# First mixer rebuilt: modulation as feature columns on turned tokens, full-row weight loads, linear attention's projections first

## What is computed

```python
mod = jax.nn.silu(c) @ w_ada[l] + b_ada[l]
sh1, sc1, gt1, sh2, sc2, gt2 = [m[:, None, :] for m in jnp.split(mod, 6, axis=-1)]
h = rms_norm(x, g_pre_mix[l]) * (1 + sc1) + sh1
y = hybrid_mixer(h, w_in[l], w_gla_gate_up[l], b_gla_gate[l], g_gla_norm[l], sinks[l], w_out[l])
x = x + gt1 * rms_norm(y, g_post_mix[l])
...
def hybrid_mixer(h, w_in, w_gla_gate_up, b_gla_gate, g_gla_norm, sinks, w_out):
    proj = h @ w_in
    aq, ak, av, gq, gk, gv, gg, ga = split_cols(proj, IN_SPLITS)
    att = sliding_window_sink_attention(...)
    glog = jax.nn.log_sigmoid((ga @ w_gla_gate_up + b_gla_gate).astype(jnp.float32)) / GLA_GATE_NORMALIZER
    o = gla_chunked(...)
    o = rms_norm(o, g_gla_norm).reshape(B, S, GLA_V_WIDTH).astype(h.dtype) * jax.nn.silu(gg)
    return jnp.concatenate([att.astype(h.dtype), o], axis=-1) @ w_out
```

## Time and profile before

| | before |
|---|---|
| median of three runs | 1823.8 us (1819.25 to 1826.76) |
| the profiled execution's own time | 1822.55 us |
| its span, first to last instruction | 1820.8 us |
| TensorE busy | 1702.5 us (94%) |
| VectorE, ScalarE busy | 670.8 us (37%), 494.4 us (27%) |
| moved from HBM | 575.06 MB, 316 GB/s over the span |
| end of the first mixer's last product | 210.7 us into the span |
| first expert pass | 259.2 us into the span |
| last expert pass ends | about 1246 us into the span |

### The profile page before, as it was taken

How to read it: one execution, slowest core, us unless ns; L and a number is a source line. 1 busy time by engine, 2 the same in 40 slices (tenths; PEclk the granted TensorE clock), 3 DMA queues, 4 the chain that set the end, 5 groups by cost and what they waited for, 6 DMA issues and landing times.

```text
span 1820.8 us, 22575 instructions
## 1 busy us (share of the span) xinstructions
PE 1702.5 (94%) x9016; PEld 960.6 (53%) x9016; DVE 670.8 (37%) x975; ACT 494.4 (27%) x696; POOL 23.1 (1%) x55
## 2 busy tenths in 40 slices
PE   4987679999999999999999999997999999999998
PEld 0873533333333333333333333335999887789997
DVE  2544532222121221212222121216555556765554
ACT  2333302121111211112121111114333444453333
POOL 2000100000000000000000000000000000000000
PEclk8898769999999999999999999998999999999999
DMA  9665739999999999999999999996655563446551
GB/s 358 210 221 208 284 149 429 428 429 428 429 429 428 429 428 429 429 428 430 427 429 429 428 430 428 428 428 216 201 186 183 178 212 117 162 148 202 185 184 68
DMA packets 117739, 576.74 MB, mean 317 GB/s; under 512 B 8016, under 2 KB 66416, under 8 KB 91328
## 3 DMA queue, kind: packets, MB, share of 16 engines
q1 hardware_dynamic: 113440, 564.22, 77.4%
q0 software_dynamic: 2512, 9.28, 1.5%
q10 hardware_dynamic: 1744, 2.63, 0.4%
HBM read 575.06 MB, written 1.05 MB: 316 GB/s over the span
## 4 chain that ended last, share of the span: by engine, by line
PE 65%; DMA 24%; DVE 7%; ACT 2%; issue 2%; DVEq 0%; SPq 0%; ACTq 0%
DMA ring<-in_w_mlp 22%; PE PS L627 22%; PE PS L912 18%; PE PS L899 7%; PE PS L969 6%; PE PS L669 3%; PE PS L892 1%; PE PS L860 1%; DMA ring<-in_w_ada 1%; PE PS L564 1%; PE PS L877 1%; DVE scr L1848 1%; DVE scr L1854 1%; DVE scr L1851 1%; PE PS L906 1%
## 5 line engine op out<-in xcount | busy, mean ns | idle before, releaser
L912 PE MATMUL PS<-ring,scr 128*64 128x512 f32 x2176 | 501.8, 615 | 9.1 <-DMA ring<-in_w_mlp 9.1
L912 PEld LDWEIGHTS PS<-ring,scr 128*64 128x64 f32 x2176 | 149.3, 135 | 342.9 <-issue 313.4
L1878 DVE TENSOR_TENSOR w_lo<-ring,w_hi 128x2048 fp32r<-128x2048 f32 x90 | 206.2, 2291 | 140.3 <-ACT w_hi L1370 140.0
L899 PE MATMUL PS<-ring,scr 128*64 128x512 f32 x1088 | 248.5, 598 | 0.0
L627 PE MATMUL PS<-HT_hi,w_hi 128*128 128x256 f32 (+1 forms) x784 | 223.4, 285 | 2.6 <-DVE HT_lo L1563 2.6
L627 PE MATMUL PS<-HT_hi,w_lo 128*128 128x256 f32 (+1 forms) x784 | 222.8, 284 | 0.0
L627 PE MATMUL PS<-HT_lo,w_hi 128*128 128x256 f32 (+1 forms) x784 | 222.7, 284 | 0.0
L1370 ACT ACTIVATE w_hi<-ring 128x2048 fp32r<-128x2048 f32 x90 | 172.2, 1913 | 169.8 <-PE PS L627 101.0
L1319 ACT ACTIVATE scr<-scr 64x512 f32<-64x512 f32 x68 | 42.3, 623 | 494.8 <-DVE scr L1847 494.8
L1836 DVE TENSOR_SCALAR scr<-iota,scr 128x128 f32<-128x128 f32 (+1 forms) x68 | 20.5, 343 | 416.1 <-PE PS L912 416.1
L1847 DVE TENSOR_SCALAR scr<-PS 64x512 f32<-64x512 f32 x68 | 46.4, 683 | 336.8 <-PE PS L912 335.6
(11 more groups left out here) (313 smaller groups left out, 1673.9 us busy)
## 6 DMA issues: line engine op xcount, KB each, us to landing
ring<-in_w_mlp SPq DMA_DIRECT2D x204, 2048.0 KB, 21.5
ring<-in_w_ada SPq DMA_DIRECT2D x24, 1024.0 KB, 11.2
ring<-in_ffn_w_gate SPq DMA_DIRECT2D x22, 1024.0 KB, 5.3
ring<-in_ffn_w_up SPq DMA_DIRECT2D x22, 1024.0 KB, 5.3
ring<-in_ffn_w_down SPq DMA_DIRECT2D x22, 1024.0 KB, 4.8
ring<-in_w_in SPq DMA_DIRECT2D x19, 1024.0 KB, 5.1
ring<-in_w_out SPq DMA_DIRECT2D x8, 1024.0 KB, 5.3
ring<-in_w_gate SPq DMA_DIRECT2D x8, 1024.0 KB, 5.1
```

The source lines that it names most:

```text
L899: mm = pe.matmul(PS[c * CAP:(c + 1) * CAP, 6, :], aT[:, h, k, :], w[:, k, c * HALF:(c + 1) * HALF], start=(h == 0 and k == 0), stop=(h == ...
L912: mm = pe.matmul(PS[c * CAP:(c + 1) * CAP, 4 + h, :], xsT[:, 2 * (j % 2) + k, j // 2, :], w[:, k, h, c, :], start=False, stop=(j == 3 and ...
L1878: dve.tensor_tensor(w_lo[:, at % PAIRS, :], raw(n), w_hi[:, at % PAIRS, :].bitcast(F32), ALU.subtract).then_inc(lo_ready, 1)
```

## The change

1. Modulation parts are taken in pairs: a chunk of `w_ada` is now one row block of 2048 columns (128 x 2048, 8 KB in one piece per partition, where it was two pieces of 4 KB), and one pair of parts is eight chunks. There are 24 chunks as before. `ada_part` does four products per chunk as before.
2. Parts 0 and 1 no longer become rows on all partitions. `c`, the gain and the two bias rows are loaded as 32 short rows and turned once by TensorE; the sums are turned by four products (L747), so that shift and scale are columns over the features. The tokens are turned first, after the bare `rsqrt` scale, and the scale and shift are then one VectorE instruction for each block of 128 features (L1703), followed by the two halves of the split. The first projection takes the feature blocks one by one as they come.
3. Parts 2 to 5: the spreading product uses a row of ones and one partition of `apart` instead of `pick`. `apart` exists three times. The products of parts 2 to 5 (16 chunks) stand in the gaps of attention's units 2 to 5, and their sums between the chunks of `w_out`.
4. The projections' order: linear attention's queries, gate, keys and values first, with its steps between the further projections; then attention, with the two chunks of the output gate in units 0 and 1. Values and output gate are taken as half-row chunks with 512 columns per product (24 products a chunk) instead of 48 with 256.
5. `w_out` is taken in the order 2, 3, 0, 1, with waits for the two kinds of head apart.
6. The raw ring has five slots instead of seven, and there are three `w_hi`/`w_lo` pairs instead of two; the memory is the same. The experts' first loads wait for the slots that lie below them, so four of the first six now wait for the end of `w_out`, where it was three.
7. Pool makes `ident` before its small loads, and loads the experts' biases only after the last modulation sum.

```diff
-RAW1, PAIRS1 = 7, 2
+RAW1, PAIRS1 = 5, 3
...
-        def chunks_mix1():
-            ada = lambda m: [two_rows(w_ada, j, m * D) for j in range(4)]
-            win = [columns(w_in, 256 * c) for c in range(5)] + [columns(w_in, 2304, RANK)] + \
-                [columns(w_in, 256 * c) for c in range(5, 9)]
-            return ada(0) + ada(1) + win[:3] + ada(2) + win[3:] + ada(3) + ada(4) + ada(5) + \
-                [two_rows(w_out, j) for j in range(4)]
+        ADA = lambda i, ks=range(KC): [("ada", i, k) for k in ks]
+        PROJ = [("gq",), ("ga",), ("gk",), ("gv", 0), ("gv", 1), ("akv",), ("aq", 0), ("aq", 1), ("gg", 0), ("gg", 1)]
+        OUT = [("out", 2), ("out", 3), ("out", 0), ("out", 1)]
+
+        LOAD1 = ADA(0, range(5)) + PROJ[:2] + ADA(0, range(5, KC)) + PROJ[2:] + ADA(1) + ADA(2, range(4)) + \
+            OUT[:2] + ADA(2, range(4, KC)) + OUT[2:]
+        USE1 = ADA(0) + PROJ + ADA(1) + ADA(2) + OUT
...
+            def ada_part(i, ks, bank):
+                for k in ks:
+                    n = in1("ada", i, k)
                     arrived(n)
+                    for g in range(4):
+                        mm = pe.matmul(PS[32 * g:32 * g + 32, bank, :], cb[:, k, :], raw(n)[:, g * HALF:(g + 1) * HALF],
+                                       start=(k == 0), stop=(k == KC - 1))
                     mm.then_inc(weights_used, 1)
...
+            ada_part(0, range(5, KC), 0)
+            pe.wait_ge(ada_sb, 1)
+            for s in range(4):
+                mm = pe.transpose(PS[:, 1, s * P:(s + 1) * P], apart[0][:, s * P:(s + 1) * P], ident[:])
+            mm.then_inc(ada_ps, 1)
+            hi, lo = split(in1("gq"), 8)
+            for k in range(KC):
+                pe.wait_ge(ht_lo, k + 1)
+                for b, bank in enumerate((0, 3)):
+                    cols = slice(b * P, (b + 1) * P)
+                    for x, w in ((HT1_hi, hi), (HT1_hi, lo), (HT1_lo, hi)):
+                        mm = pe.matmul(PS[:, bank, 0:S], w[:, k, cols], x[:, k, :], ...)
...
+            def beside(u):
+                if u < 2:
+                    two_tiles("gg", u, 0)
+                    if u == 0:
+                        pe.wait_ge(gla_dve, G_OG)
+                else:
+                    i, part = u // 2, u % 2
+                    pe.wait_ge(ev1_act, 2 + i)
+                    ada_part(i, range(4 * part, 4 * part + 4), i - 1)
+            attention(0, beside)
...
+            out_rows(2)
+            ada_sum(3)
+            out_rows(3)
+            ada_sum(4)
+            pe.wait_ge(s_olo, 2)
+            out_rows(0)
+            ada_sum(5)
+            out_rows(1)
...
+            for k in range(KC):
+                dve.tensor_scalar(vb[:, k, :], PS[:, 4 + k // 2, (k % 2) * S:(k % 2 + 1) * S], gsT[:, k:k + 1],
+                                  mod0[:, k:k + 1], ALU.mult, ALU.add).then_inc(v_ready, 1)
+                if k:
+                    low_token(k - 1)
```

More of the change, by code:

```diff
@@ L1249, in _ @@
-            attention(0, HT1_hi, project)
             act.wait_ge(gla_pe, 1)
@@ L1617, in probs @@
                     dve.tensor_tensor(s3, s3, inv.unsqueeze(2).to_broadcast([P, nh, W]), ALU.mult).then_inc(s_p[z], 1)
-                masked(0)
-                masked(1)
+                for u in range(2):
+                    masked(u)
+                    first(u)
                 for u in range(NU):
```

448 lines of the change are left out of this document (240 added, 208 removed).

## The result

| | before | after |
|---|---|---|
| median (4 runs each) | 1823.6 us | 1807.1 us (1803.5 to 1809.3) |
| the profiled execution's own time, its span | 1822.55, 1820.8 us | 1809.33, 1807.2 us |
| first projection product | 52.5 us | 37.5 us |
| T, end of the last `w_out` product | 210.7 us | 194.4 us |
| first expert pass | 259.2 us | 243.9 us |

The ratio of after to before is 0.991, 95% interval 0.988 to 0.994: faster by 16.5 us between the medians, 13.2 us between the two profiled executions. The forecast was 1801.0, with a range of 1791 to 1812; the time lies in the range, but 1.1 us above the forecast's own part of it (1797 to 1806) and so in rival B's (1806 to 1813). T is read here as the start of ScalarE's first square over the mixer's output, 0.02 us after the last `w_out` product.

A forecast was written before the change was run, and what follows sets the result against it. The mixer's end T was taken to set the experts' start, with the DMA pacing front and late modulation. Steps summed to T 189.4 against 210.7, a gain of 21.3 us from 1822.55: 1801.2, forecast 1801.0 us, range 1791 to 1812.

The forecast's parts named there:

- rival B: Whole mixer: more waits than counted, from slow landing, low clock and uncovered vector steps; T 195 to 201, 1806 to 1813 us; chance 0.19.
- the 1809 us: All loads at 358 GB/s per core: late modulation 4.3 us more, the front 4 more; set aside in favour of the trace.
- The front: Start to first projection: last first-set chunk lands at 29.5 us, 5.5 more to first product at 35.0, first chunk done at 43.3.
- The middle: Projections, linear attention and first two attention units: 51.4 us to 94.7, then 19.0 to 113.7, vector work of linear attention covered.
- The late modulation: From 113.7 us: full ring stops loads from about 91, then 13 chunks land at the DMA's pace until 150.0; last used at 151.8.
- The tail: Last attention unit, turns, modulation sums, four `w_out` chunks at 5.3 us each and a 2.2 us wait: 37.6 us, T 189.4.
- The low clock after 165 us: Sign of being wrong: TensorE's clock low after 165 us, with `w_out` expected from 161 to 189.
- Cost (a): Rate of 8 KB `w_ada` rows: taken as 409 GB/s; at 429 T is 2.3 us less; slow `w_in` pieces, T 6 us more.
- Cost (d): Experts' late biases, issued some 6 us before T and needed 11 us after: 0, at worst 3 us.
- Cost (c): TensorE's clock from linear attention on: full in the sum; at its low level in 90 to 105 us T is 197.
- rival D: Attention through `w_out`: clock stays low; T 227, 1839 us, or T 212 with only the tail low; chance 0.05.
- the step to the first expert pass: From T to the first expert pass: 48.5 us, unchanged; growth was named as a sign of being wrong.

The follow-up runs named there:

- e9: The change with GpSimd's five small loads issued only after the last first-set chunk is used: last first-set chunk landed at 29.66 us, T 190.6, 1805.8 us (one run).
- the eight: The eight kernels with the change's front (the change, e1 to e6 and e8): last first-set chunk landed at 31.4 to 32.6 us, first projection product at 35.9 to 37.9.
- e1: The change with seven raw slots and two pairs of halves in place of five and three: T 215.1 us, median 1828.7 us, ratio 1.003 to the kernel before.
- e8: As e1, with VectorE's third modulation row ahead of pair 12 and the fourth ahead of pair 13: T 195.5 us, 1812.6 us (one run).
- e2: The change with each of the 16 late modulation chunks loading only its first 128 of 2048 columns: T 177.5 us, total not comparable.
- e3: The change with the second `w_out` split (pair 11) moved behind the mixed heads' copies and low halves, third modulation row ahead of pair 12: T 194.7, median 1808.3 us.
- e6: As e5, with `w_out` chunks loaded and split earlier, beneath attention units 2 to 4, two modulation rows ahead of the last low half, root table loaded before T: 1795.7 us.
- e4: The change with one more ScalarE square root behind the last split, to load its table there: first expert pass 47.8 us after T, 1802.4 us (one run).
- e11: e6 with e9's later small loads and the narrow gate chunk loaded behind the last first-set chunk: T 179.5, median 1792.4 us, ratio 0.983 to the kernel before.
- e5: The change with the first eight late modulation chunks loaded and used between the projections, the other eight beneath attention units 2 to 5: T 187.1, median 1800.1 us.
- e7: The change with each `w_ada` chunk loaded by two transfers of 1024 columns (4 KB rows) instead of one of 2048: T 194.6, median 1810.9 us.

## Why the prediction was right, and where it was off

The mechanism was the one forecast, each piece in its place and somewhat later: first product at 37.5 us (forecast 35), scores of attention from 96.4 (93), no loads until 116 (114), DMA at full rate until 151 (150), then the tail. For the profiled execution the sum was 5.0 us short at T and 8.1 us short at the end (1801.2 against 1809.3); against the median it is 6.1 us. The time is in rival B's part of the range, but not by rival B's way: of its slow landing, low clock in linear attention and uncovered vector steps none came.

| step of the sum | predicted | measured | off |
|---|---|---|---|
| last first-set chunk landed | 29.5 | 32.6 | +3.1 |
| from there to the first product | 5.5 | 4.9 | -0.6 |
| first projection chunk | 8.3 | 7.4 | -0.9 |
| projections and linear attention, to two units' scores | 51.4 | 52.6 | +1.2 |
| output gate and two units, to the first late chunk | 19.0 | 18.5 | -0.5 |
| late modulation | 38.1 | 39.3 | +1.2 |
| tail, to T | 37.6 | 39.1 | +1.5 |
| **T** | **189.4** | **194.4** | **+5.0** |
| T to first expert pass | 48.5 | 49.5 | +1.0 |
| from there to the end of the span | 0 | | +1.7 |
| around the span | 0 | | +0.4 |

One figure came near the measured time by luck: the 1809 us that the prediction had worked out for loads at 358 GB/s. The DMA ran at 420 GB/s in the late modulation, and what my sum lacked was lost elsewhere.

**The front** was the largest single error. I had let the DMA start at 2.8 us and then run at 409 GB/s, and read the dip of the first slices as a slow start. It is not: GpSimd's 0.1 MB of small pieces cost 1.7 to 2.9 us, as e9 showed, by an estimate seven to twelve times what their bytes would take at 424 GB/s. The sum had them at nothing; with them moved away the landing is 29.66 us, where the sum has 29.5. A part of the 3.1 us is chance, since after has the latest landing of the eight. The dip was in the kernel before, too (231 and 319 GB/s in 6 to 8 and 8 to 10 us), and I did not ask for its cause. The clock was better than I had left it: 1.00 in 28 to 34 us, where I had 0.50.

**The middle** was right. The cover for linear attention's vector work held: TensorE waited 2.7 us for halves there, as in the sum, and for nothing else until the attention. It held with three pairs; with two (e1, e8) TensorE waited 6.8 us there. The sign that I had set, more than 6 us of waits for VectorE or ScalarE between 45 and 113 us, did not show: they are 3.6 us.

**The late modulation** was right in cause and in size, and e2 shows the cause. What I had wrong is the picture of it as a row of 13 transfers with a tail behind. It is a chain through the slots, and the tail hangs on it: e3 took the visible wait away and gained nothing, e6 shortened the chain and gained.

**The tail** came out within 1.5 us, and that is luck, since four errors cancel. The last unit, the turns and the first sum took 4.9 us (9.0 in my sum, which had them at the low clock), the three other modulation sums 3.2 (5.2). Against that stand the four `w_out` chunks with 26.1 us (21.2), namely two that ran in part at the low clock with 7.2 and 7.33, and two with 5.8 where I had 5.3, and the waits with 4.8 (2.2). The low clock after 165 us, which the prediction named as a sign that it is wrong, did show for these two chunks: the term that was wrong here is four chunks at 5.3 us, all at the full clock, and the low clock cost some 3 us of it.

**Cost (a)**: the row of 8 KB did give the higher rate, 420 GB/s against 401. The 358 GB/s that I had set against the trace are, as the Trainium skill also says (HBM Reference, Specifications (TRN2)), a core's share when both cores of a pair stream; a core alone gets about 425. The stretches of after agree, with 420 and 422. I had taken the figure for the wrong case. **Cost (d)**, the late biases, was nothing in after, and 1.6 us in e8. **Cost (c)** and rival D: the clock was 1.00 in 95 to 115 us and low only from about 135 on (0.66, 0.82, 0.50 in the next stretches of 5 us), where TensorE waited for chunks anyway, and in parts of the first two `w_out` chunks. The Trainium skill's rule that bursts of products between waits for DMA bring the clock back down (TensorE: Matmul & The Clock Gate, HAM oscillation) agrees with 140 to 155 us of this trace (TensorE busy 4.96 of 10 us, then 3.58 of 5, clock 0.66 and 0.50); in 120 to 135 us, with waits for chunks too (TensorE busy 11.47 of 15 us), the clock stayed at 1.00.

**After T** I had said that nothing changes, and the step to the first expert pass, which I had named as a sign of being wrong if it grew, grew by 1.0 us. The root's table had moved: the order of ScalarE's functions is part of what a change moves, and I had followed only its waits. The table is worth about a microsecond (e4, e6, e11). Before, the root's table was there already, and the first root began 0.3 us after the square ended. Of the 1.7 us lost from the first expert pass to the end I don't know the cause. About 2 us are missing in e6_all too (29.9 us earlier at the pass, 27.9 in the span) and in e11_best (31.0 and 28.7). It need not be the change: the same instructions from the first expert pass to the end of the span take 1561.6 us before, and in the eleven kernels with the same passes from 1559.9 (e4) and 1560.4 (e5) to 1564.0 (e7).

## What to carry to other kernels

A queue that stands still because its ring is full is to be looked for ahead of the stretch in which it is the limit: here 20 us without a transfer stood right before 30 us at full rate. Loading half of the late chunks earlier, beneath busy TensorE time, gained 7 us without a byte less, although the standstill itself stayed: what counts is how many transfers are left behind it. Where a ring slot is held by a step of another engine, follow the chain through slot, load and step, not the longest wait; a wait that is taken away there may only move. And a list that fixes the order of several engines fits one depth of its buffers: change the depth, and the order must be written again (20 us between e1 and e8).

## What the runs showed of the hardware that I had not expected

Small pieces: 0.1 MB of loads, the smallest pieces 4 bytes, brought the DMA from 409 to 430 GB/s down to 216 to 334 for 6 us, and the loads that they stood beside came 1.7 to 2.9 us later (e9). `w_ada` in one transfer per chunk with rows of 8 KB ran at 420 GB/s, in two with rows of 4 KB at 401 (120 to 140 us of after and e7). TensorE's clock fell again inside a run of products: in after it was 0.76 in 175 to 180 us with TensorE busy all the time, after a pause of 0.95 us, and the chunk took 7.33 us instead of 5.76. The same front landed up to 1.2 us apart between kernels that differ only behind it.
